# Feed-forward in four groups of 4, 4, 6 and 8 tiles, with block products from the fifth tile on

## The reference, cut to what matters

```python
def _conv_ffn(x, buf, w_up, conv_w, conv_b, w_down):
    u, v = jnp.split(x @ w_up, 2, axis=-1)
    uc, new_buf = _causal_dwconv(u, buf, conv_w, conv_b)
    h = jax.nn.gelu(uc.astype(jnp.float32)) * v.astype(jnp.float32)
    return h.astype(x.dtype) @ w_down, new_buf.astype(buf.dtype)

x = _layernorm(DEEPNORM_ALPHA * x + f, p['ln_ffn_g'][layer], p['ln_ffn_b'][layer])
```

## Time and profile before

| | us |
|---|---|
| median of three runs | 1370.75 |
| the profiled execution's own time | 1370.75 |
| its span, first to last instruction | 1369.0 |
| TensorE busy | 1350.6 |
| VectorE busy | 956.0 |
| ScalarE busy | 722.5 |
| GpSimd busy | 137.7 |

### The profile page before, as it was taken

The page is one execution under the profiler, slowest core; times in us unless marked ns, Lnnn a source line. Parts: engine busy times, 40 slices in busy tenths (PEclk is TensorE's granted clock), DMA queues, the critical chain, the costliest instruction groups (busy, mean ns, idle before and its releaser), DMA issues.

```text
span 1369.0 us, 24924 instructions
## 1 busy us (share of the span) xinstructions
PE 1350.6 (99%) x9900; PEld 1322.2 (97%) x9900; DVE 956.0 (70%) x1499; ACT 722.5 (53%) x1137; POOL 137.7 (10%) x146
## 2 busy tenths in 40 slices
PE   9999999999999999999999999999999999999996
PEld 8999899999999999999999999999999999999996
DVE  6656675665778558834886778878784688458865
ACT  5443544453564356623663577655652466246734
POOL 0020111100420000000000320022300000000002
PEclk9999999999999999999999999999999999999998
DMA  8175597859622345533554258853598955235522
GB/s 318 61 255 179 126 217 210 226 137 290 172 67 73 93 131 161 173 91 109 162 162 143 74 189 194 234 139 93 178 205 227 247 162 177 85 116 162 170 62 86
DMA packets 80899, 217.49 MB, mean 159 GB/s; under 512 B 6928, under 2 KB 9232, under 8 KB 80528
## 3 DMA queue, kind: packets, MB, share of 16 engines
q1 hardware_dynamic: 52560, 138.83, 31.4%
q0 software_dynamic: 27648, 76.03, 23.1%
q10 hardware_dynamic: 576, 1.05, 0.2%
HBM read 208.25 MB, written 74.74 MB: 207 GB/s over the span
## 4 chain that ended last, share of the span: by engine, by line
PE 92%; DVE 5%; DMA 1%; ACT 1%; issue 1%; SPq 0%; DVEq 0%; ACTq 0%
PE PS L770 28%; PE PS L771 28%; PE PS L772 28%; DMA raw<-weights 1%; PE PS L1098 1%; PE PS L958 1%; DVE Y L1897 1%; PE PS L964 1%; PE PS L898 1%; DVE Y L1885 1%; PE PS L919 1%; PE PS L938 1%; PE PS L942 0%; PE PS L868 0%; PE PS L928 0%
## 5 line engine op out<-in xcount | busy, mean ns | idle before, releaser
L770 PE MATMUL PS<-xhi,whi 128*128 128x296 f32 (+1 forms) x1536 | 469.7, 306 | 1.7 <-DVE wlo L1610 1.4
L771 PE MATMUL PS<-xlo,whi 128*128 128x296 f32 (+1 forms) x1536 | 458.2, 298 | 0.0
L772 PE MATMUL PS<-xhi,wlo 128*128 128x296 f32 (+1 forms) x1536 | 457.9, 298 | 0.0
L1132 ACT ACTIVATE whi<-raw 128x1024 fp32r<-128x1024 f32 (+2 forms) x256 | 253.8, 994 | 200.4 <-PE PS L772 193.4
L1604 DVE TENSOR_TENSOR wlo<-raw,whi 128x1024 fp32r<-128x1024 f32 (+2 forms) x256 | 294.1, 1152 | 65.8 <-ACT whi L1132 56.5
L770 PEld LDWEIGHTS PS<-xhi,whi 128*128 128x128 f32 x1536 | 290.3, 189 | 6.0 <-issue 2.2
L771 PEld LDWEIGHTS PS<-xlo,whi 128*128 128x128 f32 x1536 | 290.9, 189 | 1.4
L772 PEld LDWEIGHTS PS<-xhi,wlo 128*128 128x128 f32 x1536 | 289.9, 189 | 0.0
L770 PE MATMUL PS<-hhi,whi 128*128 128x296 f32 (+2 forms) x864 | 258.1, 299 | 0.4 <-DVE Y L1822 0.4
L771 PE MATMUL PS<-hlo,whi 128*128 128x296 f32 (+2 forms) x864 | 256.9, 297 | 0.0
L772 PE MATMUL PS<-hhi,wlo 128*128 128x296 f32 (+2 forms) x864 | 256.2, 297 | 0.0
(11 more groups left out here) (273 smaller groups left out, 1668.5 us busy)
## 6 DMA issues: line engine op xcount, KB each, us to landing
raw<-weights SPq DMA_DIRECT2D x118, 512.0 KB, 4.2
weight_sums<-weights POOLq DMA_DIRECT2D x24, 2048.0 KB, 16.9
raw<-weights SPq DMA_DIRECT2D x96, 256.0 KB, 3.3
weight_sums<-weight_sums POOLq DMA_DIRECT2D x8, 2048.0 KB, 11.1
raw<-weight_sums SPq DMA_DIRECT2D x64, 256.0 KB, 3.4
raw<-weight_sums SPq DMA_DIRECT2D x32, 512.0 KB, 4.0
raw<-weights SPq DMA_DIRECT2D x16, 384.0 KB, 3.2
Y<-xP SPq DMA_DIRECT2D x8, 296.0 KB, 7.3
```

The lines of the kernel that those rows point to most:

```text
L770: pe.matmul(dst, wh, h, start=first, stop=False, skip_group_check=onto)
L771: pe.matmul(dst, wh, lo, start=False, stop=False, skip_group_check=onto)
L772: return pe.matmul(dst, wl, h, start=False, stop=last, skip_group_check=onto)
L1132: act.activation(high(u, i)[:, 0:n], raw_of(u, i), ACT.Copy).then_inc(w_hi, 1)
```

## The change

There are four groups, [4, 4, 6, 8], and pairs from tile 4 on. Tiles 4 and 5 become one more block in each layer. There is one more pass of eight down units in each layer. The sums of weights now come in three groups per layer, of 4, 6 and 8 pairs; the first two of layer 0 are still made during its mixer, the third behind layer norm 0, the others behind layer norms 1 and 2. The fourth set of input sums, `input_sums(3)`, moves from tile 4 into the first and second down unit of group 0. `lambda_rows` moves to the first down unit of group 1. The first two down units of each group are interleaved (`two_down_tiles`): both go through all but the last tile or two of h, and then each through those.

```diff
--- before.py
+++ after.py
@@ -35,7 +35,7 @@
 PAST = 4096
 DFF = 2816
 FT = DFF // P
-GROUPS = [6, 8, 8]
+GROUPS = [4, 4, 6, 8]
 ALPHA = float((2.0 * 2) ** 0.25)
 EPS = 1e-5
 LRU_C = 8.0
@@ -57,7 +57,7 @@
 U_ALL = U_FFN1 + N_FFN
 
 
-SINGLE = 6
+SINGLE = 4
 SUM_STEPS = [(0, "a21", False), (1, "a11", False), (0, "a22", True), (1, "a21", True),
              (2, "s1", False), (2, "a11", True), (3, "s2", False), (3, "a12", True)]
 
@@ -115,6 +115,11 @@
             ("output", -1), ("sample", 1), ("mean", 1), ("moment", 3), ("steps", 3), ("norm", 5)]
 R_LAST = {"sample": 0, "mean": 0, "moment": 2, "steps": 2, "norm": 4}
 
+ALL_STEPS = range(len(SUM_STEPS))
+SUMS_BEHIND = [[(2, step) for step in ALL_STEPS],
+               [(3, step) for step in ALL_STEPS] + [(4, step) for step in ALL_STEPS[:4]],
+               [(4, step) for step in ALL_STEPS[4:]] + [(5, step) for step in ALL_STEPS]]
+
 
 def schedule():
 
@@ -186,7 +191,8 @@
 PLACE_OF = {place: n for n, place in enumerate(PLACES)}
 PAIRS = [u for u in range(U_ALL) if kind_of(u) in ("a", "p")]
 PER_LAYER = len(PAIRS) // 2
-PER_GROUP = PER_LAYER // (len(GROUPS) - 1)
+GROUP_OF = [layer * (len(GROUPS) - 1) + FFN[u - base][2] - 1 for layer, base in enumerate((U_FFN0, U_FFN1))
+            for u in PAIRS if base <= u < base + N_FFN]
 RAWS = 4
 
 
@@ -612,7 +618,7 @@
                     sp.dma_start(to[:, 0:n], weights[u, :, 0:n]).then_inc(loaded, 16)
                     return
                 n = PAIRS.index(u - second(u))
-                sp.wait_ge(w_sums[n // PER_GROUP], 16 * len(SUM_STEPS))
+                sp.wait_ge(w_sums[GROUP_OF[n]], 16 * len(SUM_STEPS))
                 if second(u):
                     if i:
                         sp.dma_start(to[:, first], weights[u, :, last]).then_inc(loaded, 16)
@@ -675,9 +681,9 @@
             def sum_step(group, step):
 
                 first, last = slice(0, HALF), slice(HALF, 2 * HALF)
-                n = group * PER_GROUP
-                units = weights[PAIRS[n]:PAIRS[n] + 2 * PER_GROUP].rearrange("(n t) p c -> t p n c", t=2)
-                sums = W_SUMS[n:n + PER_GROUP].rearrange("n p c -> p n c")
+                n, count = GROUP_OF.index(group), GROUP_OF.count(group)
+                units = weights[PAIRS[n]:PAIRS[n] + 2 * count].rearrange("(n t) p c -> t p n c", t=2)
+                sums = W_SUMS[n:n + count].rearrange("n p c -> p n c")
                 to, source, add = SUM_STEPS[step]
                 source = {"a11": units[0][:, :, first], "a12": units[0][:, :, last], "a21": units[1][:, :, first],
                           "a22": units[1][:, :, last], "s1": sums[:, :, 0:HALF],
@@ -746,9 +752,8 @@
                     low_row(ln, 0, m)
                 for m in range(KT):
                     low_row(ln, 1, m)
-                if ln:
-                    for step in range(len(SUM_STEPS)):
-                        sum_step(1 + ln, step)
+                for group, step in SUMS_BEHIND[ln]:
+                    sum_step(group, step)
             for i in range(3):
                 for of_square in (False, True):
                     add_second_half(3, i, of_square)
@@ -799,6 +804,24 @@
                         side(u, k)
                         if both:
                             side(u + 1, k)
+
+            def two_down_tiles(u, late, k0):
+
+                n = unit_tiles(u)
+                for ks in (range(n - late), range(n - late, n)):
+                    for i in range(2):
+                        for k in ks:
+                            pe.wait_ge(h_lo, k0 + k + 1)
+                            cols = slice(k * P, k * P + P)
+                            if k == 0:
+                                weights_ready(pe, u + i)
+                                pe.wait_ge(free[(u + i) % 2], (u + i) // 2)
+                            for half in range(2):
+                                t = span(half, off(u + i))
+                                mm = products(acc[(u + i) % 2][:, half, 0:wid(u + i)], high(u + i)[:, cols],
+                                              low(u + i)[:, cols], hhi[:, k, t], hlo[:, k, t], k == 0, k == n - 1)
+                            if k == n - 1:
+                                mm.then_inc(full[(u + i) % 2], 1)
 
             def half_product(u, half, k, hi, lo, signal=None, third=None, norm=None):
 
@@ -1069,8 +1092,11 @@
                         last_tiles(ub + i, 2 * layer + 1)
                     elif i > N_FFN - 4:
                         pass
+                    elif kind == "d" and j == 0:
+                        two_down_tiles(ub + i, 2 if g else 1, FT * layer + first)
                     elif kind == "d":
-                        gemm(ub + i, hhi, hlo, h_lo, FT * layer + first)
+                        if j > 1:
+                            gemm(ub + i, hhi, hlo)
                     elif i == 0:
                         first_tiles(ub, 2 * layer)
                     elif i > 1 and ub + i not in THIRD:
@@ -1449,7 +1475,9 @@
                         act.wait_ge(free[u % 2], u // 2 + 1)
                         done(act.activation(hhi[:, j - first, at:], s(4 + j % 2, at), ACT.Copy), h_hi)
                     else:
-                        if layer == 0 and g == 0 and j == 0:
+                        if g == 0 and j == 0:
+                            input_sums_hi(KT // 2 - 1)
+                        if layer == 0 and g == 1 and j == 0:
                             done(act.activation(lam[:, 0:KT], par("lru_lambda", 0, KT), ACT.Abs))
                             done(act.activation(lam[:, 0:KT], lam[:, 0:KT], ACT.Exp, scale=-1.0), lam_a)
                         if g == len(GROUPS) - 1 and j < KT - 4:
@@ -2106,7 +2134,11 @@
                              h_lo)
                     elif kind == "d":
                         add_tile(u, j, g == 0, 2 * layer + 1 if g == len(GROUPS) - 1 else None)
-                        if layer == 0 and g == 0 and j == 0:
+                        if g == 0 and j == 0:
+                            input_sums(KT // 2 - 1)
+                        elif g == 0 and j == 1:
+                            input_sums_lo(KT // 2 - 1)
+                        if layer == 0 and g == 1 and j == 0:
                             lambda_rows()
                     if kind == "u" and 1 <= j <= KT // 2:
                         input_sums(j - 1)
```

## The result

The changed kernel took 1381.44 us (median of 4 runs, 1380.10 to 1384.39), the kernel before on the same chip 1370.91. The ratio is 1.0078, with a 95% interval from 1.0066 to 1.0090: 10.5 us slower, and 4 us above the upper end of the range. The forecast was 1372.5. The profiled execution is the slowest of the four, 1384.39 us (span 1382.5), so the comparison of spans, 13.5 us, has to account for some 3 us more than the medians show.

A forecast was written before the change was run, and what follows sets the result against it. TensorE, busy 99% of the span, was taken as the bound. Saved matmuls and new waits, -6.5 + 2.4 + 2.6 + 3.2 = +1.7 us on 1370.75, gave 1372.5 us, called no change; range 1368.0 to 1377.5.

The forecast's parts named there:

- The saved matmuls: Tiles 4 and 5 as a block, 168 matmuls instead of 192: 3.42 us less in layer 0, 3.05 in layer 1.
- Group 0's pass: Down pass of group 0: TensorE waits behind VectorE and ScalarE queues, 2.4 us in layer 0, 2.6 in layer 1.
- the three waits 0.37, 0.36 and 1.70: Layer 0, group 0's down pass: second unit's bank 0.37 us late, third unit's bank 0.36, fourth unit 1.70.
- Group 1's pass: Layer 0, group 1's down pass: lambda_rows behind the first addition makes the fourth unit wait 3.2 us; layer 1 nothing.
- pays for itself: Layer 0, group 1's down pass: interleaved, tiles 2 and 3 are in time; otherwise tile 2 is wanted at 1.64 us.
- GpSimd's steps: Behind layer norm 1, twelve steps for 56 pairs against 64, free for layer norm 2 about as early: nothing added.
- rival (a): Loads starve beside sum steps in two blocks per layer: up to 5.5 us each, 5 taken, 1377.5 us; chance 0.17.
- Behind layer norms 0 and 2 it issues more: GpSimd issues more sum steps behind these norms; left out of the sum and treated as the starving-loads rival.

The follow-up runs named there:

- e11_spread: Changed kernel with lambda_rows at group 2, group 0's queues reordered, head steps spread over seven heads, other sum steps mostly kept off blocks: 1364.74 us, ratio 0.9958.
- e4_queues: Changed kernel with ScalarE's, VectorE's and the first unit's work reordered at group 0's down pass, both layers: 1377.01 us, ratio 1.0042 to the kernel before.
- e1_lambda: Changed kernel with lambda_rows moved from group 1's down pass to group 2's: 1374.99 us, ratio 1.0035 to the kernel before.
- e6_short_lambda: Changed kernel with four of eight series terms left out of lambda_rows, in its old place: 1377.29 us, ratio 1.0044 to the kernel before.
- e2_sums_early: Changed kernel with sum steps of groups 3 and 4 behind layer norm 0, group 5 behind norm 1, none behind norm 2: 1375.76 us, ratio 1.0041.
- e9_plain_downs: Changed kernel with the interleaving undone, each down unit going through its tiles by itself: 1379.92 us, ratio 1.0072 to the kernel before.
- e8_interleave_only: Kernel before with only the first two down units of each group interleaved, groups of 6, 8 and 8 tiles kept: 1374.86 us, ratio 1.0026.
- e3_head_steps: Changed kernel with the last sum step of groups 0 and 1 issued behind layer norm 0 instead of in layer 0's mixer: 1378.75 us, ratio 1.0058.
- e5_all: Changed kernel with lambda_rows at group 2, group 0's queues reordered, later sum steps issued earlier, head steps spread over seven heads: 1367.04 us, ratio 0.9975.

## Why the prediction was wrong

**The saved matmuls, -6.5.** Right. Undisturbed, layer 1's feed-forward part takes 381.94 us (e11_spread) against 384.83 before, 2.9 where 3.05 was forecast, and two blocks take 45.56 us in layer 0 (changed kernel) and 45.01 in layer 1.

**Group 0's pass, +2.4 and +2.6.** Right: 2.2 and 2.35. Of the three waits 0.37, 0.36 and 1.70, the first two measured 0.29 and 0.30, the third 1.37 (a gap less one spacing). e4_queues, by reordering the queues, takes all three away, so the cause was the queues, as counted.

**Group 1's pass, +3.2.** The wait was right (3.10), its price wrong: TensorE's granted clock fell to 1.2 GHz for 3.4 us behind it, 1.7 us more. The step had no term for what a wait does to the matmuls behind it, and the longest wait in dense matmuls of the kernel before is 1.85 us from start to start, so its trace had no case of it. e1_lambda and e6_short_lambda bear out what made the wait. The 1.7 us is not due each time: in e2_sums_early the same wait cost only itself.

**What the interleaving does.** I priced it at +0.37 and "pays for itself" in group 1. e9_plain_downs agrees that it makes hardly a difference over the changed kernel as a whole. But I held it harmless in general: e8_interleave_only shows that it pulls the first two additions together, and that this cost 4 us in the kernel before.

**GpSimd's steps, rival (a), chance 0.17.** This is the step that failed first: the overlap of loads and sum steps in layer 1 was put at nothing in the sum. Its mechanism was worked out, with its place (two whole blocks) and price (up to 5.5 us per layer), and then set at 5 for both layers and held unlikely, because no wait showed on TensorE before. But no wait is no cushion measured: the share of 1.05 beside a block stood in the earlier trace rows. Layer 1 lost 7.0 in the profiled execution (3.3 to 5.1 in three others; e2_sums_early loses none of it), layer 0 none. My picture of the place was too narrow as well: the two blocks lost only 1.7, the pass behind them 0.3 and the three blocks behind that 4.9, since the last step was issued at 1134.65 and landed at 1156.6.

**The output projection, not in the sum, +3.6.** "Behind layer norms 0 and 2 it issues more" looked only behind the norms. That groups 0 and 1 now share out 4 and 6 pairs instead of 8 in the head's eight steps was read as less work. e3_head_steps and e5_all, which issue neither step there, show that these two delay the loads of the output projection: 2.75 us of waiting against 0.67, and the clock behind it. That it is their going out together that costs more than before rests on the two traces; no run keeps both and sets them apart. Why the second step went out 20 us later before stays open: the profile puts 18.61 us down to "issue", and the one wait that the kernel has between the two, for the group's own step before, had been over since 321. The trace of before shows the same at all four accumulating pairs, so a reader of it could have seen that smaller steps may move; whether the bytes of a step decide it, no run tests.

Sum as measured in the profiled execution: -6.5 + 2.2 + 2.35 + 3.1 = +1.2, near the forecast +1.7; then 1.7 (clock), 3.6 and 7.0 that it did not have: 13.5. The medians differ by 10.5; that layer 1 lost less in the other executions would account for it, but they have no trace.

## What to carry to other kernels

A change that saves the bounding engine a per cent shifts everything that was tuned to hide behind it, so go through each queue that feeds it, over the whole span and not only near the edit, and ask how far ahead it is; a trace without waits doesn't say. Bulk transfers beside loads are a matter of place: the same steps cost up to 7 us or nothing. And a wait of some 2 to 3.5 us on a busy TensorE should be given a chance of costing 1.7 us beyond itself: here it did in 12 cases of 15.
